# A two-layer hybrid attention trunk on one core: five changes of order and hand-over between engines

## The chip, the core and the metric

The kernel runs on one core of one Trainium2 chip. The core has a matrix engine (TensorE, PE in the profile, with its weight loads as PEld), a vector engine (VectorE, DVE), a scalar engine (ScalarE, ACT), a general engine (GpSimd, POOL) and a queue engine (SyncE, SP) that issues most of the DMA transfers. The engines run side by side and wait for each other by semaphores. The metric is the device time of one execution in microseconds (us).

## The reference, cut to what matters

Everything is float32. The sequence has 1,024 tokens, the model is 1,024 wide, and there are two layers with weights of their own.

```python
for i in range(2):                                   # DEPTH
    hn = rmsnorm(h, attn_norm[i])
    qkv = hn @ w_qkv[i]                              # 1024 x 2304
    # group A: 8 query heads, 2 key heads of 64; own chunk of 64 and the one before;
    # QK-norm, rotary on a quarter of the head, and a learned sink in the softmax
    ya = softmax(concat([scores_a, sink]))[..., :-1] @ v_a
    # group B: 8 heads of 64; own chunk and 8 before; QK-norm and a learned relative bias
    yb = softmax(scores_b + bias) @ v_b
    h = h + concat([ya, yb]) @ w_o[i]                # 1024 x 1024
    h = h + conv_gated_mlp(rmsnorm(h, ffn_norm[i]))  # up 1024 x 5632, conv of 3, silu gate, down 2816 x 1024
    gate = sigmoid(rmsnorm(h, ple_norm[i]) @ w_ple_gate[i])
    h = h + (p[i] @ w_ple_proj[i]) * gate
```

## The kernel before

A Fori loop over the two layers (L) stands on every engine, and the order of the work on each engine is written out by hand. Engines hand over by counting semaphores; a few waits name a later count than they need, by a constant at the top (C_GATE, C_HEADS and others are added to a semaphore once at the start, so that waits of the first layer have the same form). The 1,024 tokens are 8 tiles of 128 (TT), and the 1,024 columns are 8 blocks of 128 (KT). Each float32 product is three matmuls: the operands are split into a high part, which ACT writes (functions with "high"), and a low part, which DVE or POOL writes (functions with "low"), and high x high, high x low and low x high are summed in PSUM.

A layer has these stages, with their place in the first layer of the profiled span; the second layer runs about 1,293 us later.

1. Transposes of h (7 to 24 us). `transpose_x` transposes 8 x 8 tiles by matmuls with `ident` (L2001). Banks of PSUM hold four blocks; for block k at 4 or above PE waits until DVE's `x_low` (L1504) has emptied the bank of block k - 4. ACT's `x_high` (L1003) comes ahead of it. When the source is h, tiles 0 to 5 go first for blocks 0 to 3, each as soon as it is loaded; in the second layer all of them wait for the gate's last additions (L1985) of the layer before, by `s_gate_added`.
2. qkv projection (24 to 225 us), in 6 chunks of 384 columns (L2025 to L2027).
3. Attention B (225 to 355 us): 8 heads x 8 items. An item is a tile of queries of one head. Per item PE makes scores (L2134), DVE adds the bias and keeps the negated maximum (`add_bias`, L1593), ACT takes the exponential (L1098), PE transposes the probabilities (L2164), DVE or ACT copies them (L1614, L1118) and PE multiplies by v (L2183). `fill_high` and `fill_low` (L1572) make a head's q and k operands, four fills for a head of B.
4. Attention A (355 to 425 us), the same with 8 heads x 8 items. The softmax's sink: DVE adds `sink_g` and `neg_max` (L1678), ACT takes the exponential of the sum in place, and DVE's `finish` adds it to the denominator (L1628), takes the reciprocal (L1631) and scales the head's output into `qkv` (L1634).
5. Output projection (425 to 515 us): `transpose_x` of the heads' outputs once all 16 heads are done (`s_head_done`), then the products with w_o, whose rows SP loads in eight pieces (`load_o`) of 256 rows.
6. Up projection with conv and gate (515 to 965 us): products over units (L2335 to L2338); ACT and DVE put the products' results together (`c11`, `c12`, `c22`, the copy at L1395).
7. Down projection (965 to 1190 us): 42 batches of up to 24 matmuls (L2359 to L2361), whose operands `ad` and `bd` come from ACT's `ad_high`, `bd_high` (L1327, L1340) and DVE's `ad_low`, `bd_low` (L1893, L1898).
8. Gate (1190 to 1302 us): ACT's sigmoid (L1443), and DVE's product and sum into h (L1981, L1985), 16 of each, the last for tile 7.

ACT functions live in tables: `table(f)` (L973) makes a small activation that brings in the table. Here the Sqrt table comes in at the start of each layer, ahead of `x_high`.

## Time and profile before

| | |
|---|---|
| median of 3 runs (lowest, highest) | 2606.36 us (2606.30, 2608.78) |
| the profiled execution: time, span | 2602.32 us, 2600.4 us |
| PE busy, share of the span | 2551.1 us, 98% |
| PEld, DVE | 2195.6 us (84%), 1382.0 us (53%) |
| ACT, POOL | 1300.4 us (50%), 1015.2 us (39%) |
| mean granted clock of TensorE | 0.998 |
| chain that ended last | PE 93%, DVE 3%, issue 2%, ACT 1%, POOL 1% |

The span runs from the first to the last instruction of the profiled execution; its time is 1.9 us longer, and it was a little faster than the median of the three runs. Busy times are sums over all instructions of an engine, so the engine with the largest share is not at work only where that pays; the rows further down show single places.

### The profile page before, as it was taken

The numbers are of one execution on the slowest core, as the hardware profiler recorded it, in microseconds if no ns is written. First come the engines' busy times: TensorE is split into PE (matmuls) and PEld (weight loads), VectorE is DVE, ScalarE is ACT, GpSimd is POOL, SyncE is SP. The second block draws the span as 40 slices with busy tenths as digits, with TensorE's granted clock in tenths as the row PEclk, the third lists the DMA queues.
The fourth block names the chain that finished last, engine by engine and source line by source line (L and its number), as shares of the span: only waits on it lengthen the run. The fifth ranks groups of instructions, "written<-read, shape, count | busy, mean of one in ns | idle before, by whom it ended". The sixth has DMA issues, their size and how long they took to land.

```text
span 2600.4 us, 41681 instructions
## 1 busy us (share of the span) xinstructions
PE 2551.1 (98%) x13328; PEld 2195.6 (84%) x13328; DVE 1382.0 (53%) x2057; ACT 1300.4 (50%) x2156; POOL 1015.2 (39%) x749
## 2 busy tenths in 40 slices
PE   8999999999999999999999999999999999999999
PEld 8999988777888878887899999887778888788877
DVE  3114675176556567872331156742766566777732
ACT  4335775275555553333343367742755555533342
POOL 3454221238787750001124442201388787400011
PEclk9999999999999999999999999999999999999999
DMA  4111000223233248431111110003233333473312
GB/s 159 43 48 42 27 2 18 89 66 119 79 112 114 77 156 293 130 105 41 37 43 43 49 35 27 2 18 104 66 105 93 104 105 103 164 277 120 98 49 81
DMA packets 179768, 223.84 MB, mean 86 GB/s; under 512 B 7952, under 2 KB 110736, under 8 KB 179632
## 3 DMA queue, kind: packets, MB, share of 16 engines
q1 hardware_dynamic: 179040, 219.66, 26.4%
q0 software_dynamic: 592, 2.46, 0.3%
q8 instruction: 74, 1.21, 0.2%
q14 instruction: 62, 0.51, 0.1%
HBM read 169.08 MB, written 55.36 MB: 86 GB/s over the span
## 4 chain that ended last, share of the span: by engine, by line
PE 93%; DVE 3%; issue 2%; ACT 1%; POOL 1%; DMA 0%; DVEq 0%; ACTq 0%; SPq 0%; POOLq 0%
PE ps L2025 10%; PE ps L2027 10%; PE ps L2026 10%; PE ps L2335 10%; PE ps L2338 10%; PE ps L2337 10%; PE ps L2359 6%; PE ps L2361 5%; PE ps L2360 5%; PE ps L2183 5%; PE ps L2134 3%; PE ps L2164 3%; PE ps L2109 2%; PE ps L2001 1%; DMA h<-in_x 0%
## 5 line engine op out<-in xcount | busy, mean ns | idle before, releaser
L807 POOL TENSOR_TENSOR w_hl<-w_raw,w_hl 128x1024 fp32r<-128x1024 f32 x84 | 201.4, 2398 | 1039.4 <-ACT w_hl L981 1039.4
L2025 PE MATMUL ps<-w_hl,xT 128*128 128x384 f32 (+1 forms) x1280 | 461.2, 360 | 0.3
L2027 PE MATMUL ps<-w_hl,xT 128*128 128x384 f32 (+1 forms) x1280 | 460.0, 359 | 0.0
L2026 PE MATMUL ps<-w_hl,xT 128*128 128x384 f32 (+1 forms) x1280 | 460.0, 359 | 0.0
L981 ACT ACTIVATE w_hl<-w_raw 128x1024 fp32r<-128x1024 f32 x84 | 89.0, 1059 | 460.8 <-PE ps L2027 436.2
L2025 PEld LDWEIGHTS ps<-w_hl,xT 128*128 128x128 f32 x1280 | 240.2, 188 | 24.7 <-DVE xT L1504 1.5
L2027 PEld LDWEIGHTS ps<-w_hl,xT 128*128 128x128 f32 x1280 | 240.2, 188 | 23.5
L2026 PEld LDWEIGHTS ps<-w_hl,xT 128*128 128x128 f32 x1280 | 240.2, 188 | 23.3
L1836 DVE SCALAR_TENSOR_TENSOR ps<-c_up,ccols,ps 128x1023 f32<-128x1023 f32 x84 | 107.8, 1283 | 151.8 <-ACT ps L1292 151.8
L1521 DVE TENSOR_REDUCE q_sum<-sq 128x384 f32 x80 | 44.2, 553 | 271.4 <-ACT sq L1038 271.4
L1098 ACT ACTIVATE probs<-scores,neg_max 128x192 f32<-128x192 f32 (+5 forms) x256 | 144.3, 565 | 39.9 <-DVE neg_max L1593 39.3
L2359 PE MATMUL ps<-bd_two,ad 128*128 128x512 f32 x392 | 155.2, 396 | 2.8 <-DVE bd_two L1898 2.8
L1815 DVE TENSOR_TENSOR c_up<-ps,kept 128x512 f32<-128x512 f32 x126 | 86.6, 688 | 130.7 <-DMA v_rows<-hc_g 70.3
L2361 PE MATMUL ps<-bd_two,ad 128*128 128x512 f32 x392 | 154.9, 395 | 0.0
L2360 PE MATMUL ps<-bd_two,ad 128*128 128x512 f32 x392 | 154.8, 395 | 0.0
L2134 PE MATMUL ps<-ks,qs 128*128 128x192 f32 (+4 forms) x640 | 134.3, 324 | 3.1 <-DVE neg_max L1593 3.1
L1327 ACT ACTIVATE ad<-ad_raw 128x1024 fp32r<-128x1024 f32 x84 | 82.8, 986 | 105.4 <-DMA ad_raw<-v_rows 102.9
L2335 PE MATMUL ps<-x_four,ring_three 128*128 128x512 f32 x336 | 131.6, 392 | 3.4 <-POOL ring_three L919 3.4
L2335 PE MATMUL ps<-x_four,ring_four 128*128 128x512 f32 x336 | 133.2, 397 | 1.6 <-ACT kept L1251 1.5
L2338 PE MATMUL ps<-x_four,ring_four 128*128 128x512 f32 x336 | 133.0, 396 | 0.0
L2337 PE MATMUL ps<-x_four,ring_four 128*128 128x512 f32 x336 | 132.8, 395 | 0.0
L919 POOL TENSOR_TENSOR ring_four<-t_sum,ring_four 128x512 fp32r<-128x512 f32 x82 | 115.6, 1409 | 43.3 <-ACT ring_four L1178 42.1
(270 smaller groups left out, 6272.9 us busy)
## 6 DMA issues: line engine op xcount, KB each, us to landing
ad_raw<-v_rows SPq DMA_DIRECT2D x70, 512.0 KB, 3.7
raw_a<-in_w_up SPq DMA_DIRECT2D x44, 512.0 KB, 4.9
raw_g<-in_w_up SPq DMA_DIRECT2D x44, 512.0 KB, 5.2
v_rows<-c_up SPq DMA_DIRECT2D x22, 1024.0 KB, 4.4
w_raw<-in_w_qkv SPq DMA_DIRECT2D x48, 384.0 KB, 3.2
wd_main<-in_w_down SPq DMA_DIRECT2D x30, 512.0 KB, 7.8
v_rows<-hc_g SPq DMA_DIRECT2D x22, 512.0 KB, 5.0
w_raw<-in_w_o SPq DMA_DIRECT2D x16, 512.0 KB, 3.3
```

The source lines that it names most:

```text
L807: nc.gpsimd.tensor_tensor(w_hl[:, slot % 2, 1, :], w_raw[:, slot % 2, :], w_hl[:, slot % 2, 0, :].bitcast(F), ALU.subtract) \
L1098: nc.scalar.activation(buffer(probs, kind, n)[:, c0:c0 + keys], buffer(scores, kind, n)[:, c0:c0 + keys], ACT.Exp, bias=neg_max[:, hp, t:t ...
L2025: nc.tensor.matmul(dst, lhs[:, k, 0, cols], wh, start=first, stop=False)
L2026: nc.tensor.matmul(dst, lhs[:, k, 0, cols], wl, start=False, stop=False)
L2027: return nc.tensor.matmul(dst, lhs[:, k, 1, cols], wh, start=False, stop=last)
L2134: done = nc.tensor.matmul(score_bank(kind, n)[:, c:c + w], qs[:, hd % 2, t * P:(t + 1) * P], ks[:, kv(kind, hd), part, k0 + c:k0 + c + w], ...
L2335: nc.tensor.matmul(dst, wh, xs[:, 0, k], stop=False, skip_group_check=True, start=k == 0 and (q in (1, 2, 5) or (v, q) == (UNITS - 1, 4)))
L2337: nc.tensor.matmul(dst, wh, xs[:, 1, k], start=False, stop=False, skip_group_check=True)
L2338: mm = nc.tensor.matmul(dst, wl, xs[:, 0, k], start=False, stop=k == 3, skip_group_check=True)
L2359: nc.tensor.matmul(d_bank(n, t), xh[:, e, cols], wh[:, e], start=k == 0 and e == 0, stop=False)
L2360: nc.tensor.matmul(d_bank(n, t), xh[:, e, cols], wl[:, e], start=False, stop=False)
L2361: mm = nc.tensor.matmul(d_bank(n, t), xl[:, e, cols], wh[:, e], start=False, stop=k == STEPS_OF - 1)
```

## The change

It makes five edits.

- **Down's first batch.** ACT and DVE make `ad` and `bd` of batch 0 ahead of the last copy (L1395) and the last `c22` of the up projection, where they came behind them.
- **The first bias of attention.** At the start of B, DVE adds the bias of item 0 ahead of the fourth fill. At the start of A, it makes the two fills of the next head behind the biases of items 4 and 5, where they stood ahead.
- **Sink by ACT alone.** DVE's sum (L1678) goes; ACT's exponential reads `neg_max` and takes `sink_g` as its bias.
- **B rows first at the output projection.** Transposes and w_o's rows come in the order B, A. PE waits for B's heads before block 0 and for all heads only before block 3.
- **Layer boundary and table.** The Sqrt table comes in before the loop and at the end of each layer. PE starts a layer's transposes when 14 of the 16 gate additions are in, and waits for all before block 3; the early tiles take blocks 0 to 2, where they took 0 to 3.

```diff
-        C_LOW, C_USED, C_SUMS, C_HEADS, C_GATE = 2, 2, 2, 2, 2
+        C_LOW, C_USED, C_SUMS, C_HEADS, C_GATE = 2, 2, 2, 2, 4
@@ SP
                     sp.wait_ge(s_w_low_ready, L * SLOTS + i * c + (slot + 1))
+                    if O0 <= slot < P0:
+                        settled(sp)
                     sp.dma_start(dst, src).then_inc(raw_loaded[slot % 2], 16)
...
                 def load_o(j):
+                    first = 256 * ((j + 2) % 4)
@@ ACT
             act.wait_ge(s_first_loaded, 32)
+            table(ACT.Sqrt)
             with act.Fori(0, DEPTH) as L:
...
-                table(ACT.Sqrt)
                 x_high(0, 0, {1: 0, 5: 1})
...
                         if kind == "A" and t == TT - 2:
 
-                            act.wait_ge(s_den_part, L * A_HEADS + (hd + 1))
-                            nc.scalar.activation(sink_e[:, hd % 2, :], sink_e[:, hd % 2, :], ACT.Exp) \
-                                .then_inc(s_sink_exp, 1)
+                            act.wait_ge(s_scores_biased, item(hd * TT + TT - 1))
+                            nc.scalar.activation(sink_e[:, hd % 2, :], neg_max[:, hd % 2, :], ACT.Exp,
+                                                 bias=sink_g[:, hd:hd + 1], scale=1.0).then_inc(s_sink_exp, 1)
...
                 keep_s2(0, 0, last)
+                ad_high(0)
+                bd_high(0)
                 act.wait_ge(s_u_done, L * PRODUCTS + product_number(last, 7))
                 act.wait_ge(s_combined, L * COMBINED + combined_number(last, "C11"))
                 nc.scalar.activation(c_up[1][:, 0, HALF:], bank_of(last, 7), ACT.Copy).then_inc(s_kept, 1)
-                for b in range(2):
-                    ad_high(b)
-                    bd_high(b)
+                ad_high(1)
+                bd_high(1)
...
                     if n == 0:
                         high(P0 + 6)
+                table(ACT.Sqrt)
@@ DVE
                     if first and kind == "B":
-                        for f in range(len(fills(kind, 0))):
+                        for f in range(3):
                             fill_low(0, f, True)
-                        for n in range(lead_s):
+                        add_bias(0)
+                        fill_low(0, 3, True)
+                        for n in range(1, lead_s):
                             add_bias(n)
                     if first:
                         for n in range(lead_t):
                             copy_p(n)
-                        if kind == "A":
-                            for f in range(2):
-                                fill_low(1, f)
...
                             for m in within(n + lead_s):
                                 add_bias(m)
+                            if n == 0:
+                                for f in range(2):
+                                    fill_low(1, f)
...
-                        if kind == "A" and t == 4:
-
-                            dve.wait_ge(s_scores_biased, item(hd * TT + TT - 1))
-                            nc.vector.tensor_scalar(sink_e[:, hd % 2, :], neg_max[:, hd % 2, :], sink_g[:, hd:hd + 1],
-                                                    None, ALU.add).then_inc(s_den_part, 1)
...
                 c12(0, 0, last)
+                dve.wait_ge(s_combined, L * COMBINED + combined_number(last, "C12"))
+                ad_low(0)
+                bd_low(0)
                 dve.wait_ge(s_kept, L * COPIES + copy_number(last, "own"))
                 c22(0, 0, last)
-                dve.wait_ge(s_combined, L * COMBINED + combined_number(last, "C12"))
                 for b in range(BATCHES):
-                    ad_low(b)
-                    bd_low(b)
+                    if b:
+                        ad_low(b)
+                        bd_low(b)
@@ PE, transpose_x and its calls
                         ready(t)
-                        for k in range(4):
+                        for k in range(3):
                             one(t, k)
...
-                        for t in range(early if k < 4 else 0, TT):
+                        for t in range(early if k < 3 else 0, TT):
...
-                pe.wait_ge(s_gate_added, L * 2 * TT + C_GATE)
-                transpose_x(0, lambda t, k: h[:, t, k * P:(k + 1) * P],
+                def every_tile(k):
+                    if k == 3:
+                        pe.wait_ge(s_gate_added, L * 2 * TT + C_GATE)
+
+                pe.wait_ge(s_gate_added, L * 2 * TT + (C_GATE - 2))
+                transpose_x(0, lambda t, k: h[:, t, k * P:(k + 1) * P], every_tile,
...
-                pe.wait_ge(s_head_done, L * 16 + 16 + C_HEADS)
-                transpose_x(KT, lambda t, k: qkv[:, t, (k * P if k < 4 else B_Q + (k - 4) * P):
-                                                 (k * P if k < 4 else B_Q + (k - 4) * P) + P])
+                def every_head(k):
+                    if k == 3:
+                        pe.wait_ge(s_head_done, L * 16 + 16 + C_HEADS)
+
+                pe.wait_ge(s_head_done, L * 16 + B_HEADS + C_HEADS)
+                transpose_x(KT, lambda t, k: qkv[:, t, (B_Q + k * P if k < 4 else (k - 4) * P):
+                                                 (B_Q + k * P if k < 4 else (k - 4) * P) + P], every_head)
```

The program's listing shows each engine's instructions in their order; ISA and REGISTER_ALU rows belong to waits and counters. First DVE where attention B begins, before the change (L1572 is a fill, L1593 the bias of an item, whose keys are 128 for item 0 and 256 for item 1):

```order
L1572 SCALAR_TENSOR_TENSOR qs<-ps,qk_cols,qs 64x512
L1564 REGISTER_ALU
L1572 SCALAR_TENSOR_TENSOR ks<-ps,qk_cols,ks 128x512
L1572 SCALAR_TENSOR_TENSOR qs<-ps,qk_cols,qs 64x512
L1583 ISA
L1586 REGISTER_ALU
L1593 ISA scores,neg_max<-ps,bias 128x128
L1593 ISA neg_max 128x1
L1586 REGISTER_ALU
L1593 ISA scores,neg_max<-ps,bias 128x256
```

And with the change (L1576 and L1597 are the same lines there):

```order
L1576 SCALAR_TENSOR_TENSOR qs<-ps,qk_cols,qs 64x512
L1568 REGISTER_ALU
L1576 SCALAR_TENSOR_TENSOR ks<-ps,qk_cols,ks 128x512
L1587 ISA
L1590 REGISTER_ALU
L1597 ISA scores,neg_max<-ps,bias 128x128
L1597 ISA neg_max 128x1
L1576 SCALAR_TENSOR_TENSOR qs<-ps,qk_cols,qs 64x512
L1590 REGISTER_ALU
L1597 ISA scores,neg_max<-ps,bias 128x256
```

The bias of item 0 now stands ahead of the last fill; that of item 1 stands where it stood.

ACT between the up and the down projection, before (c_up is written by the copy of the last product, `ad` and `bd_two` are batch 0's operands, then `ad` and `bd_one` batch 1's):

```order
L1395 ACTIVATE c_up<-ps 128x512
L1326 REGISTER_ALU
L1327 ACTIVATE ad<-ad_raw 128x1024
L1333 ISA
L1337 REGISTER_ALU
L1340 ACTIVATE bd_two<-wd_main 128x1024
L1326 ISA
L1327 ACTIVATE ad<-ad_raw 128x1024
L1340 ACTIVATE bd_one<-wd_main 128x1024
```

With the change:

```order
L1329 ACTIVATE ad<-ad_raw 128x1024
L1335 ISA
L1339 REGISTER_ALU
L1342 ACTIVATE bd_two<-wd_main 128x1024
L1397 REGISTER_ALU
L1398 REGISTER_ALU
L1399 ACTIVATE c_up<-ps 128x512
L1328 ISA
L1329 ACTIVATE ad<-ad_raw 128x1024
L1342 ACTIVATE bd_one<-wd_main 128x1024
```

Batch 0's two activations have moved ahead of the copy and its waits.

PE at the start of a layer, before (32 transposes follow one wait; after them, 8 by 8, come those that wait for DVE's `x_low`):

```order
L1995 ISA
L2001 MATMUL ps<-ident,h 128x128 x32
L2014 ISA
L2001 MATMUL ps<-ident,h 128x128 x8
L2014 REGISTER_ALU
L2001 MATMUL ps<-ident,h 128x128 x8
```

With the change:

```order
L1999 ISA
L2005 MATMUL ps<-ident,h 128x128 x24
L2057 REGISTER_ALU
L2005 MATMUL ps<-ident,h 128x128 x8
L2018 ISA
L2005 MATMUL ps<-ident,h 128x128 x8
L2018 REGISTER_ALU
L2005 MATMUL ps<-ident,h 128x128 x8
```

A second wait (L2057, for all 16 additions) now stands behind 24 transposes, and the 8 of block 3 follow it.

## Rows read from the trace of the kernel before

**Rows 1.** PE's waits over the whole span: us in total, times, longest us

```profile
PE ps L2164 <- ACT probs L1098: 6.0, 7, 1.1
...
PE ps L2359 <- DVE bd_two L1898: 2.8, 2, 1.4
PE ps L2001 <- DVE qkv L1634: 2.6, 2, 1.3
```

**Rows 2.** Timeline of ACT, DVE and PE between up and down projection: start, duration, idle before

```profile
962.55 0.60 ACT L1395 ACTIVATE c_up<-ps 128x512 f32<-128x512 f32 x1 [4.95 <-PE ps L2338]
...
963.36 0.69 DVE L1815 TENSOR_TENSOR c_up<-ps,kept 128x512 f32<-128x512 f32 x1 [2.91 <-ACT c_up L1395]
...
965.27 1.22 DVE L1898 TENSOR_TENSOR bd_two<-wd_main,bd_two 128x1024 fp32r<-128x1024 f32 x1
...
966.63 0.47 PE L2359 MATMUL ps<-bd_two,ad 128*128 128x512 f32 x1 [1.40 <-DVE bd_two L1898]
```

**Rows 3.** DMA issues between 952 and 954.8: KB each, us to landing

```profile
ad_raw<-v_rows SPq DMA_DIRECT2D x1, 512.0 KB, 6.5
...
wd_main<-in_w_down SPq DMA_DIRECT2D x1, 512.0 KB, 6.2
```

**Rows 4.** Timeline of DVE and PE at the start of attention B

```profile
226.62 0.76 DVE L1572 SCALAR_TENSOR_TENSOR qs<-ps,qk_cols,qs 64x512 fp32r<-64x512 f32 x1 [0.73 <-ACT qs L1051]
...
227.77 0.62 PE L2134 MATMUL ps<-ks,qs 128*128 128x384 f32 x2 [1.53 <-DVE neg_max L1593]
...
229.06 0.44 PE L2164 MATMUL ps<-ident,probs 128*128 128x128 f32 x2
```

**Rows 5.** Timeline of DVE and PE at the start of attention A

```profile
356.87 1.43 DVE L1572 SCALAR_TENSOR_TENSOR qs<-ps,qk_cols,qs 64x512 fp32r<-64x512 f32 x2
358.32 0.42 DVE L1593 CUSTOM_DVE_ANT_0 scores<-ps,mask_a,neg_sink 128x192 f32<-128x192 f32 x1
...
359.38 0.88 PE L2164 MATMUL ps<-ident,probs 128*128 128x128 f32 x4 [1.14 <-ACT probs L1098]
```

**Rows 6.** The sink's sum by its line (ns min/median/max), and POOL's timeline at the first long one

```profile
L1678 DVE TENSOR_SCALAR sink_e<-neg_max,sink_g x16: 220/230/1950, 363.8 to 1715.8; 128x8 f32<-128x8 f32 x16
...
363.78 1.91 POOL L815 TENSOR_TENSOR q_nat<-qkv,q_rstd 128x1024 f32<-128x1024 f32 x1 [4.00 <-PE ps L2109]
```

**Rows 7.** Timeline of PE where three heads of attention A begin their products with v

```profile
386.32 0.88 PE L2183 MATMUL ps<-qkv,probsT 128*128 128x64 f32 x6 [0.33 <-DVE probsT L1614]
...
395.93 0.88 PE L2183 MATMUL ps<-qkv,probsT 128*128 128x64 f32 x6 [0.34 <-DVE probsT L1614]
...
404.19 0.88 PE L2183 MATMUL ps<-qkv,probsT 128*128 128x64 f32 x6 [0.34 <-DVE probsT L1614]
```

**Rows 8.** Stretches of A: length, busy PE, PEld, DVE, ACT, POOL, PE clock, DMA

```profile
1653.60:1657.10 3.50, 3.50 (x20) 3.50 (x19) 1.20 (x6) 1.01 (x2) 0.00 (x0) 0.51 0.00 0
...
359.38:368.03 8.65, 7.27 (x60) 6.40 (x60) 6.65 (x18) 5.40 (x19) 2.31 (x2) 1.00 0.00 1
1652.30:1661.21 8.91, 8.58 (x59) 7.96 (x60) 4.93 (x18) 5.42 (x19) 2.31 (x2) 0.81 0.00 1
```

**Rows 9.** Timeline of DVE and PE at the boundary of the layers

```profile
1300.57 0.69 DVE L1985 TENSOR_TENSOR h<-gate_s,h 128x512 f32<-128x512 f32 x1
...
1310.32 2.48 DVE L1504 SCALAR_TENSOR_TENSOR xT<-ps,ncols,xT 128x1024 fp32r<-128x1024 f32 x2 [6.19 <-ACT xT L1003]
...
1304.19 5.38 PE L2001 MATMUL ps<-ident,h 128*128 128x128 f32 x32 [2.31 <-DVE h L1985]
...
1316.97 0.44 PE L2025 MATMUL ps<-w_hl,xT 128*128 128x384 f32 x1
```

**Rows 10.** The loop's jump: ACT's timeline behind it; branches (ns min/median/max, first and last start)

```profile
1304.66 1.28 ACT L973 ACT_TABLE_LOAD   x1 [1.98 <-issue]
...
L976 ACTq COMPARE_BRANCH  x2: 40/42/45, 1302.1 to 2595.2; - x2
...
L1464 DVEq FUSED_REGOPS  x2: 63/65/67, 3.8 to 1306.6; - x2
```

More of the change, by code:

```diff
@@ L547, in trunk @@
         s_sinks_set = sem("sinks_set")
-        s_den_part = sem("den_part")
         s_sink_exp = sem("sink_exp")
@@ L642, in load_o @@
                 def load_o(j):
+                    first = 256 * ((j + 2) % 4)
                     load(O0 + j, 0, 0, rows2(O0 + j, HALF),
-                         tiled(w_o[ds(L, 1), 256 * (j % 4):256 * (j % 4) + 256, j // 4 * HALF:(j // 4 + 1) * HALF]))
+                         tiled(w_o[ds(L, 1), first:first + 256, j // 4 * HALF:(j // 4 + 1) * HALF]))
                 load_o(0)
```

## The prediction

> **What bounds the kernel now.** The first view read is the page's head: PE is busy 98% of the span and holds 93% of the chain that ended last. An edit therefore pays only where PE is idle or runs at its lower clock. The second is PE's waits by cause: single waits of 1.1 to 1.4 us [rows 1] and one of 2.3 between the layers [rows 9], most of them once a layer, where PE waits on another engine's order of work. The third is the timeline of the waiting engines ahead of each such wait: which instruction released PE, and what stood ahead of it. The fourth is the table of stretches, for the granted clock. The sum is made against the profiled execution (2602.32 us, span 2600.4) and then taken off the median, 2606.36 us, which is 4.0 us longer.
>
> **1. Down's first batch.** PE's first down matmul comes 1.40 us late, released by DVE's `bd_two` at 965.27 + 1.22 = 966.49 [rows 2]. That chain begins with ACT's copy at 962.55, a copy that waits 4.95 us for PE; DVE too sits idle for 2.91 us before 963.36. So both engines have free time before PE ends its last product at about 965.2 (966.63 less 1.40). The only question is whether the operands are there. Batch 0's `ad_raw` is issued after 952 and lands 6.5 us later; its weights are issued before 954.8 and land 6.2 us later, before 961 [rows 3]. With ACT's two activations (about 1 us each; the order listing puts them ahead of the copy) and DVE's two at 1.22, both parts are done by about 964.1 even if DVE starts only at 961.7. The wait goes: 1.40 in each layer, 2.8 together, as PE's waits give it for two times [rows 1]. Next late is batch 1, which DVE now makes behind `c22`, as before; a batch of 24 matmuls of 0.47 us that overlap by about half (an estimate) lasts over 5 us, so batch 1's operands, which DVE begins right behind `c22`, have some slack. **2.8 us.**
>
> **2. First bias of B.** PE waits 1.53 us at 227.77 for the bias of item 0, which stands on DVE behind a fill of 0.76 that itself came 0.73 late behind ACT [rows 4]. The order listing shows that bias moved ahead of the fill, but the bias of item 1 not. So the bias of item 0 comes 1.3 to 1.5 earlier, the upper bound. But PE's transposes of item 1 at 229.06 hang on the bias of item 1, behind the fill as before, which only saves the bias ahead of it (0.2 to 0.3), and on ACT, which then has item 0 out of its way. I take 0.5 (between 0.3 and 1.5, near the lower end, as one item alone cannot keep PE busy). **1.0 us** for two layers.
>
> **3. First bias of A.** Two fills of 1.43 us in all stand at 356.87 ahead of the bias at 358.32, and PE waits 1.14 us at 359.38 [rows 5]. With the fills behind, the bias begins at 356.87; ACT is then busy with a copy until about 357.75, so its exponential and PE's transposes come 1.05 earlier (bounds 0.6 and 1.14). The fills belong to the next head, so their new place costs nothing while that head is several us away. **2.1 us** for two layers.
>
> **4. The sink's sum.** It is 16 instructions of a median of 0.23 us on DVE, with a longest of 1.95 [rows 6]. Three are long, and the first stands right beside POOL's 1.91 us at 363.78 [rows 6]. The 13 short ones lie in idle time of DVE and cost PE nothing. A long one shows in PE's pace: the head starts at 386.32, 395.93 and 404.19 are 9.61 and 8.26 us apart [rows 7]; the first interval holds a long sum, the second none, so one costs 1.35 (lower bound 1.0, PE's idle time there by itself). What replaces it on ACT is nothing: the exponential was there before, with one wait fewer ahead of it. **4.05 us** for three.
>
> The Trainium skill (SBUF — State Buffer, SBUF: two separate sides) says that DVE and GpSimd share a pair of ports which one of them holds for a whole instruction while the other blocks. The trace agrees (1.95 against 0.23), and by that rule a sum that is gone can't collide, but another DVE instruction may meet POOL's in its place; that is rival 2.
>
> **5. The clock in layer 1's A.** TensorE's granted clock stands at its lower level (0.51, that is 1.2 GHz) from 1653.60 to 1657.10 [rows 8], right after PE's idle 1.1 us at the start of A. The same work takes 8.91 us there, and 8.65 in layer 0, where it holds one long sum [rows 8]: 8.65 − 1.35 = 7.30, so the fall costs 1.6. In layer 0 the same idle time brought no fall, so it is a matter of chance; with the idle time gone I take it as gone. **1.6 us** (bounds 0 and 1.6).
>
> **6. B rows first at the output projection.** PE waits 1.3 us, twice, for the last head's scaled output [rows 1]. B's heads are long done, so blocks 0 to 2 (24 transposes, about 2.7 us) need no wait, and only block 3 does, by then met. ACT's and DVE's copies of the transposed blocks begin as much earlier; ACT's table and DVE's last scaling are done by then. w_o's pieces change only their rows; the first two are loaded during B. SP's added instruction is one of tens of ns per load. **2.6 us.**
>
> **7. Layer boundary.** Here everything between PE's last gate matmul and its first qkv matmul at 1316.97 is a chain. Before: DVE's last addition, PE's transposes at 1304.19 after 2.31 us of waiting, DVE's first `x_low` at 1310.32, first product 6.65 after that [rows 9]. PE would now start after the addition for tile 5 (1300.57 + 0.69 = 1301.26) and its own last matmul, which ends at 1304.19 − 2.31 = 1301.88: 2.3 earlier. `x_high` needs its bank, and `x_low` needs DVE. ACT compares for its jump at 1302.1 and does its first instruction behind it, the table load of 1.28 us, at 1304.66; DVE is back in the loop only at 1306.6 [rows 10]. Neither DVE's jump nor its start moves. The table load now stands ahead of ACT's jump, from about 1302.7; the likelier case is that the jump's 2.5 us run beside it, since compare and fetch are the sequencer's work. So ACT's `x_high` can be done before 1306, and DVE's first `x_low` comes at about 1306.8 instead of 1310.3. From there on the chain has five `x_low` of 1.24 (2.48 for two [rows 9]), so the first product comes at about 1313.1: **3.9 us**, once. The lower value: if ACT's jump begins only when the table is in, at about 1304.0, its 2.5 us end near 1306.4, `x_high` and with it `x_low` come some 1.2 later, and 2.7 us are won.
>
> The Trainium skill (Runtime: NRT & Kernel Launch, Instruction fetch mechanics) states that a taken branch out of the window of fetched pages forces a transfer of the target page before execution goes on. The trace agrees: 2.5 us from compare to the next instruction on ACT. By that rule a table load ahead of the jump could not be hidden by it, and the sum would be 1.2 us smaller.
>
> The first layer's start has nothing to win, since x comes by DMA there; the table load before the loop lies beside that load, and the one at the end of the last layer beside the last stores.
>
> **Sum.** 2.8 + 1.0 + 2.1 + 4.05 + 1.6 + 2.6 + 3.9 = 18.05 us, so 2602.32 falls to about 2584.3 and the median, 2606.36, to 2588.3. That is 0.7%; 0.2% (5.2 us) is about what a measurement of this kernel can tell from no change.
>
> **The rivals.** *Forecast, all of it about as summed:* a gain of 15 to 20.5 us, 2586 to 2591.5. Its bounds are items 2, 3 and 7 at their lower values together (−0.4, −0.9, −1.2) and item 2 at its upper one (+2). Chance 0.58.
>
> *Rival 1: the boundary gives its gain back.* PE has a new gap there: it ends 32 transposes before DVE is back, so it is idle for some 2 us, and at the same kind of place the clock stood at its lower level for 3.5 us at a price of 1.6 [rows 8]. With the late jump (−1.2) and one such fall in the first products (−1.6 more): 18.05 − 2.8 = 15.2, some 2591. For it: the boundary has three engines' jumps in it. Against it: the chain there is bound by DVE and not by PE's clock until the first product. Chance 0.19.
>
> *Rival 2: the collisions move, and the fall stays.* POOL's instruction now meets another of DVE's small ones (reciprocal or sum of the denominator). Then the 4.05 and the 1.6 stay lost: 12.4 us, 2594. For it: POOL's work is placed by the same events as before, a few tenths of a us from DVE's. Against it: none of those was long in the 16 heads before, only the sink's sum. Chance 0.13.
>
> *Rival 3: waits replaced by waits.* Each wait removed uncovers one behind it, on DMA, say w_o's rows or `ad`'s second batch. If only the sink's part stays, the gain is 4 us, 2602, within 0.2%. Against it: the copies behind each wait have slack in the timeline. Chance 0.07.
>
> *Rival 4, the other side: the clock.* In A, PE has gaps (7.27 us busy of 8.65 [rows 8]). If the new spacing of its work let the clock fall to its lower level in A again and again, each fall of 3.5 us costs 1.6. Slower by over 0.2% needs 18.05 + 5.2 = 23.3 us, or 15 such falls in 16 heads; at 8 falls the gain would be 5 us and lost in the noise. One fall is in the trace, and the change makes the gaps fewer. Chance 0.03, slower and a little below that together.
>
> **How the numbers follow.** The likeliest case gives 2588.3. The range goes from 2584 (item 2 at its upper value, and 2 us for sizes of mine that are short) to 2596, which takes in rivals 1 and 2; what is left out above is rivals 3 and 4 at 0.10. Faster by over 0.2% (below 2601.1) are the forecast, rivals 1 and 2 and a little of 3: 0.91. Within 0.2%: the rest of 3 and the small side of 4, 0.07. Slower: 0.02.
>
> **What the profile after would show.** Item 1: no wait of PE on `bd_two`. Items 2 and 3: the wait on `neg_max` at 227.8 shorter, but a short one on item 1's exponential left; the 1.14 at the start of A gone or under 0.2. Item 4: no DVE instruction of 1.9 us in A, head intervals all 8.3. Item 5: clock 1.00 through layer 1's A. Item 6: the transposes from `qkv` follow the last product with v at once. Item 7: from the end of PE's last gate matmul to the first qkv matmul 11.2 us in place of 15.1 (1301.88 to 1316.97), and DVE, not ACT, ahead of `x_low`. Wrong would make it: long instructions of DVE under other names, w_o's load late at the output projection, or the lower clock in more than one stretch of A.

## The result and the profile after

The median of four executions is 2583.39 us (2583.16 to 2583.57), beside 2607.24 us for the kernel before (2606.30 to 2608.78): a measured ratio of 0.9899, interval [0.9881, 0.9917] (the two medians by themselves give 0.9909, inside it). The forecast was 2588.3 with a range of 2584 to 2596, so the time fell 0.6 us below the range. The profiled execution went from 2602.32 to 2583.39 us, 18.93 less, where 18.05 had been summed. Taken off 2606.36, even 18.93 gives 2587.4, inside the range. The step that failed is therefore not in the sum but behind it: the median moved by 23.0 from the 2606.36 that the prediction started from, and by 23.9 from 2607.24. Some of this was luck: run again, the changed kernel has a median of 2587.1, inside the range and 1.2 below the forecast (see the experiments).

PE's waits over the whole span of the changed kernel (us in total, times, longest us; its line numbers are 4 to 12 higher). The waits on `bd_two`, on `qkv` and on h's last addition are gone, and those on ACT's exponential fell from 6.0 to 0.6 [rows 1]:

```profile
PE ps L2191 <- DVE probsT L1618: 3.3, 10, 0.3
...
PE ps L2142 <- DVE neg_max L1597: 1.5, 4, 0.5
...
PE ps L2172 <- ACT probs L1100: 0.6, 2, 0.3
```

Timeline of PE at the start of B, the start of A, in A, at the output projection, and at down's first batch (start, duration, idle before and its releaser):

```profile
228.49 0.44 PE L2172 MATMUL ps<-ident,probs 128*128 128x128 f32 x2
...
357.64 0.88 PE L2172 MATMUL ps<-ident,probs 128*128 128x128 f32 x4
...
383.22 0.88 PE L2191 MATMUL ps<-qkv,probsT 128*128 128x64 f32 x6 [0.33 <-DVE probsT L1618]
...
391.49 0.88 PE L2191 MATMUL ps<-qkv,probsT 128*128 128x64 f32 x6 [0.34 <-DVE probsT L1618]
...
420.59 1.15 PE L2005 MATMUL ps<-ident,qkv 128*128 128x128 f32 x9
...
959.25 0.39 PE L2371 MATMUL ps<-bd_two,ad 128*128 128x512 f32 x1
```

Read against [rows 2, 4, 5, 7], the same rows stood at 229.06, 359.38, 386.32, 395.93 and 966.63. The lead is 0.57 us behind the first bias of B (0.19 of it from the program's start), 1.74 behind the first bias of A, 3.10 and 4.44 each time that a long sum is gone, and 7.38 behind the output projection and down together. The transposes at 420.59 follow the last product with v without a gap.

Timeline of ACT and DVE at down's first batch. The last operand of batch 0 is ready at 957.39 (956.17 + 1.22), ahead of PE's start at 959.25, and ACT's copy comes behind ACT's part of it:

```profile
955.07 1.07 ACT L1342 ACTIVATE bd_two<-wd_main 128x1024 fp32r<-128x1024 f32 x1 [0.80 <-DMA wd_main<-in_w_down]
...
956.73 0.60 ACT L1399 ACTIVATE c_up<-ps 128x512 f32<-128x512 f32 x1 [0.59 <-PE ps L2350]
...
956.17 1.22 DVE L1899 TENSOR_TENSOR bd_two<-wd_main,bd_two 128x1024 fp32r<-128x1024 f32 x1 [0.17 <-ACT bd_two L1342]
```

Timeline at the boundary of the layers, and the rows of ACT's and DVE's jump (ns min/median/max, first and last start):

```profile
1294.28 3.66 PE L2005 MATMUL ps<-ident,h 128*128 128x128 f32 x32
...
1300.69 5.23 PE L2005 MATMUL ps<-ident,h 128*128 128x128 f32 x32 [2.76 <-DVE xT L1508]
1305.68 0.42 PE L2029 MATMUL ps<-w_hl,xT 128*128 128x384 f32 x1
...
1295.18 1.28 ACT L975 ACT_TABLE_LOAD   x1
...
L979 ACTq FUSED_REGOPS  x2: 50/53/56, 3.0 to 1297.2; - x2
...
L979 ACTq COMPARE_BRANCH  x2: 40/42/45, 1294.5 to 2576.4; - x2
...
1299.35 6.05 DVE L1508 SCALAR_TENSOR_TENSOR xT<-ps,ncols,xT 128x1024 fp32r<-128x1024 f32 x5 [2.74 <-ACT xT L1006]
...
L1468 DVEq FUSED_REGOPS  x2: 63/65/67, 3.0 to 1299.1; - x2
```

PE starts its transposes with no wait at all. ACT's jump runs from 1294.5 to 1297.2, and the table load lies inside it: ACT's sequencer and its table load ran side by side, so the prediction's likelier case held, and its rule that a table load ahead of the jump could not be hidden by it did not. DVE is back at 1299.1 and starts `x_low` 0.25 us later, in one run of five. From the end of PE's last gate matmul (1294.44) to the first qkv product it is 11.2 us, as forecast; it was 15.1. Not all of that is the edit's: 1.6 us of it was a fall of the clock in the execution before, as shown further down.

One collision in each layer did move, as rival 2 had it, to the sum of the denominator (L1632, at 392.07 and 1673.87; L1628 before, whose longest was 0.17). It takes 0.78 us, and behind it the lead shrinks by 0.15 and 0.18 us:

```profile
L1632 DVE TENSOR_TENSOR den<-den,sink_e x16: 154/164/779, 365.5 to 1702.7; 128x8 f32<-128x8 f32 x16
```

### The profile page after: what moved, and what is told of

Its sections match the earlier page's. It is cut to its first block, busy times and chain, and to the rows that moved or that the text cites. A ratio compares the mean times of both kernels' runs of the same rounds, so it can differ in the third digit from the quotient of the medians.

```text
span 2581.5 us, 41681 instructions
## 1 busy us (share of the span) xinstructions
PE 2546.2 (99%) x13328; PEld 2191.5 (85%) x13328; DVE 1375.0 (53%) x2041; ACT 1303.0 (50%) x2158; POOL 1015.4 (39%) x749
## 4 chain that ended last, share of the span: by engine, by line
PE 93%; DVE 2%; issue 2%; ACT 1%; POOL 1%; DMA 0%; ACTq 0%; DVEq 0%; SPq 0%; POOLq 0%
PE ps L2029 10%; PE ps L2031 10%; PE ps L2030 10%; PE ps L2347 10%; PE ps L2350 10%; PE ps L2349 10%; PE ps L2371 6%; PE ps L2373 6%; PE ps L2191 6%; PE ps L2372 6%; PE ps L2142 3%; PE ps L2172 3%; PE ps L2117 2%; PE ps L2005 1%; DMA h<-in_x 0%
```

## The experiments

Eighteen runs were made, two of them of the unchanged kernels, most with 6 or 12 executions each. They ran in five groups, each on a chip of its own, and the kernel before ran beside each group (its median went from 2606.0 to 2613.2 us between them), so a kernel is best compared with the one before of its own group, as the ratio does. In the table, the clock is the mean over executions of the mean granted clock. Over all groups the kernel before has 122 executions: 2602.0 to 2626.0, median 2609.8, clock 0.9954.

| kernel | n | lowest, median, highest us | clock | ratio to before, interval |
|---|---|---|---|---|
| before, again | 12 | 2602.4, 2608.9, 2618.8 | 0.9959 | 0.9995 [0.9972, 1.0018] |
| changed, again | 6 | 2583.5, 2587.1, 2587.4 | 0.9993 | 0.9903 [0.9882, 0.9924] |
| sink alone | 12 | 2596.7, 2600.5, 2606.9 | 0.9978 | 0.9972 [0.9953, 0.9991] |
| bias of A alone | 12 | 2603.8, 2612.1, 2617.5 | 0.9950 | 1.0002 [0.9982, 1.0023] |
| boundary alone | 12 | 2598.6, 2603.5, 2614.5 | 0.9963 | 0.9982 [0.9961, 1.0003] |
| B's rows alone | 12 | 2600.3, 2607.5, 2617.5 | 0.9953 | 0.9988 [0.9970, 1.0006] |
| down alone | 12 | 2601.3, 2612.0, 2621.5 | 0.9934 | 0.9995 [0.9975, 1.0016] |
| sink and bias of A | 7 | 2595.1, 2597.4, 2602.0 | 0.9971 | 0.9935 [0.9912, 0.9958] |
| changed, sink's sum on DVE | 12 | 2590.7, 2596.5, 2607.5 | 0.9964 | 0.9950 [0.9933, 0.9967] |
| changed, old boundary | 6 | 2586.0, 2591.1, 2594.6 | 0.9987 | 0.9925 [0.9903, 0.9946] |
| changed, old bias of A | 6 | 2585.3, 2589.5, 2591.1 | 0.9992 | 0.9901 [0.9874, 0.9927] |
| changed, old rows | 6 | 2586.7, 2590.0, 2595.1 | 0.9995 | 0.9914 [0.9894, 0.9934] |
| changed, old bias of B | 6 | 2583.9, 2586.9, 2590.0 | 0.9988 | 0.9904 [0.9885, 0.9923] |
| changed, old down | 6 | 2590.0, 2590.7, 2594.2 | 0.9992 | 0.9918 [0.9900, 0.9937] |
| changed, DVE stalls | 12 | 2606.8, 2610.7, 2617.4 | 0.9933 | 0.9989 [0.9968, 1.0009] |
| changed, ACT stalls of 0.8 | 6 | 2587.3, 2591.0, 2595.0 | 0.9995 | 0.9918 [0.9898, 0.9938] |
| changed, ACT stalls of 1.2 | 6 | 2588.1, 2592.6, 2598.0 | 0.9985 | 0.9934 [0.9916, 0.9952] |
| changed, ACT stalls of 3.1 | 12 | 2612.2, 2614.7, 2618.6 | 0.9919 | 1.0017 [1.0004, 1.0030] |

### Spread: the kernel before and the changed one, again

No edit.

> The kernel before, unchanged, as a measure of how its executions spread. Theory C (clock): the timed executions lie above the profiled one of 2602.3 because they hold one to three more stretches at the lower TensorE clock (each 1.6 to 1.7 us), which follow PE's waits; expected: times from 2601 to 2609 in steps of about 1.7, and a lower mean clock (0.996 to 0.997) where the time is longer. Theory E (execution): the offset has nothing to do with the clock; expected: times near 2606 to 2608 at the same clock of 0.998 as the profiled one.

> The changed kernel, unchanged, for its spread. Theory P (phase): the qkv projection of a layer runs at one of two paces, 0.1733 or 0.1766 us from matmul to matmul, 3.8 us apart per layer, drawn anew in each execution, and the clock's falls come on top; the change doesn't touch the draw, and the first result (2583.2 to 2583.6) was the lucky end: expected 2583 to 2600, median 2587 to 2589, as far above the profiled execution as before. Theory R (removed): the change takes away what starts the slow pace and most falls; expected 2583 to 2586 in nearly all executions, median 2583.5, while the kernel before spreads from 2602 to 2620 on the same chip.

Measured: over all groups the kernel before spreads over 24 us, with a mean clock from 0.989 to 0.999 and longer times at a lower clock. So theory E, that the times differ at the same clock, is refuted; theory C, that the longer times come with a lower clock, holds, but its range, 2601 to 2609, is too short. The profiled execution here has four falls ahead of the end. Three of its stretches (length, busy PE, PEld, DVE, ACT, POOL, PE clock, DMA share, GB/s) are just behind waits of PE: the start of A, in A, and the output projection:

```profile
361.30:364.70 3.40, 3.40 (x19) 3.40 (x17) 1.49 (x6) 1.64 (x5) 0.00 (x0) 0.50 0.00 0
1689.10:1692.50 3.40, 3.40 (x19) 3.38 (x18) 1.62 (x6) 1.08 (x5) 0.00 (x0) 0.51 0.40 149
1719.80:1723.20 3.40, 3.40 (x17) 3.40 (x18) 0.34 (x1) 1.02 (x1) 0.00 (x0) 0.50 0.00 0
```

The changed kernel has a second thing that varies and is not the clock. Its profiled execution, 2587.36 us, has not one fall before its end, and is 3.97 us longer than the first one. Nearly all of the two layers' qkv projections, the same 1,151 matmuls, shows why:

```profile
24.13:223.24 199.11, 199.11 (x1151) 199.07 (x1152) 39.38 (x71) 77.89 (x125) 88.56 (x89) 1.00 0.20 56
1305.84:1508.75 202.91, 202.91 (x1152) 202.87 (x1153) 39.38 (x71) 78.40 (x126) 88.72 (x89) 1.00 0.18 50
```

Both at full clock and fully busy, but 3.80 us apart. Per matmul that is 0.1730 us in one and 0.1763 in the other. Of the 40 layers in the 20 profiled executions of this study, 11 ran at the slow pace, in the first layer or in the second, in kernels of both kinds.

So each theory was half right. The pace is drawn in the changed kernel too (theory P, 2583.5 or 2587.3), and the clock's falls are nearly gone from it (theory R). The six times fit it: two at 2583.5 and 2584.4, four at 2587.0 to 2587.4, as with no slow layer and with one. All of the first four executions, at 2583.2 to 2583.6, were of the first kind, and that was luck.

### Single parts on the kernel before

The sink alone, the bias of A alone, the boundary with the table alone, B's rows alone, and down alone. Each is the hunks of the change that belong to it; the core of each:

```diff
# sink
+                            nc.scalar.activation(sink_e[:, hd % 2, :], neg_max[:, hd % 2, :], ACT.Exp,
+                                                 bias=sink_g[:, hd:hd + 1], scale=1.0).then_inc(s_sink_exp, 1)
# bias of A
+                            if n == 0:
+                                for f in range(2):
+                                    fill_low(1, f)
# boundary and table
+                pe.wait_ge(s_gate_added, L * 2 * TT + (C_GATE - 2))
# B's rows
+                pe.wait_ge(s_head_done, L * 16 + B_HEADS + C_HEADS)
# down
+                ad_high(0)
+                bd_high(0)
```

> Only the sink's sum is left to ACT. By the profiled sum: 4.05 us less, 2603 beside a median of 2607. Theory C adds what falls of the clock follow the collisions of DVE with POOL: 1.6 to 3.3 us more if they cause some, none if they don't. Rival (collisions move to another small DVE instruction): 0 us, and a DVE instruction of 1.9 us under another name in A.

> Only the two fills at the start of A move behind the biases. By the profiled sum: 2.1 us less (1.05 in each layer) and 1.6 more for the clock's fall behind the wait in layer 1. Theory C: the fall at the start of A comes in many executions of the kernel before, up to one in each layer, so 3.7 to 5.4 us less in the median. Theory E: 2.1 us less.

> Only the layer boundary: 14 of 16 additions waited for, blocks 0 to 2 early, table load ahead of the jump. By the sum: 3.9 us less. If one of the two stretches of lower clock at the boundary also goes, its price lies in transposes that wait for DVE anyway, so still about 3.9. If ACT's jump begins only behind the table load: 2.7.

> The kernel before with only B's rows first at the output projection and w_o in that order. By the sum 2.6 us less than before (profile: PE's wait of 1.3 on the last head's output gone, twice). Rival: w_o's rows or the last copies late, with a wait at the first product of w_o; 0 to 1 us less. The clock fell at this place in other executions, so 1.6 more may go in each layer.

> The kernel before with only down's first batch made ahead. By the profile 2.8 us less (PE's wait of 1.40 gone in both layers). No fall of the clock was seen at this place, so the mean clock stays at that of the kernel before, 0.9957, and the best executions come to 2599. Rival (the wait moves to batch 1): 0 to 1 us less.

Measured: the profile shows each removed wait gone, but against a spread of 24 us only the sink alone is told from no change in the times: its median lies 5.6 below, where 4.05 was expected (the interval allows both), and its clock rises from 0.9957 to 0.9978. The other lowest times are 0.8 to 3.5 us below before's 2602.1, except the bias of A alone, whose lowest is 2603.8. Its profiled execution (2613.23) shows why it can't be read in the times: seven falls and one layer at the slow pace. Theory C is refuted where it gave the falls to the wait at the start of A alone; there are as many without it.

### Two parts together

The sink and the bias of A (the two diffs above).

> The kernel before with two parts, the sink's sum on ACT and the biases of A first, which leaves no wait of PE over 0.4 us inside attention A. By the profile 4.05 + 2.1 = 6.2 us less than before's executions with the same clock. Theory W (the clock falls where PE has waits of a us and more in attention): hardly a fall left in A, mean clock 0.998 to 0.999, median 2594 to 2597. Rival (each part acts by itself, and bias_a alone took no fall away): clock as with the sink alone, 0.9978, median 2598.

Measured: the lowest is 2595.1, as summed (6.2 below 2602.1 is 2595.9), and the clock, 0.9971, not above the sink's alone. That is the rival's outcome; theory W had 0.998 to 0.999. The four falls of its profiled execution are at 19.8, 422.5, 1518.2 and 1712.8 us, none inside A, but three of them where waits are left: the start of B, and the end of A in both layers.

### Single parts taken out of the changed kernel

```diff
# changed kernel with the sink's sum on DVE again
+                            nc.vector.tensor_scalar(sink_e[:, hd % 2, :], neg_max[:, hd % 2, :], sink_g[:, hd:hd + 1],
+                                                    None, ALU.add).then_inc(s_den_part, 1)
# with the old boundary
-                pe.wait_ge(s_gate_added, L * 2 * TT + (C_GATE - 2))
+                pe.wait_ge(s_gate_added, L * 2 * TT + C_GATE)
# with the old bias of A: fill_low(1, f) ahead of the loop again
# with the old rows
+                pe.wait_ge(s_head_done, L * 16 + 16 + C_HEADS)
# with the old bias of B: four fills, then the biases
# with the old down: ad_high(0), bd_high(0), ad_low(0), bd_low(0) behind the copy and c22
```

> The changed kernel with the sink's sum back on DVE. By the profile 4.05 us more than the changed kernel (2587.5 in the best executions), if the sum still meets POOL's instruction three times; the number of long sums may change as the other parts shift it: 1.35 for each. If collisions bring falls of the clock (theory R), the spread grows to that of the kernel before; by theory P it doesn't change.

> The changed kernel with the layer boundary and the table load as before. By the profile 3.7 us more (2587.1 in the best executions). Theory R, if the boundary's wait of 2.3 us and its clock fall start the slow pace in layer 2: executions at 2591 appear, 3.8 above. Theory P: as many slow executions as the changed kernel has.

> The changed kernel with the two fills again ahead of the first biases of A: PE waits 1.14 us at the start of A, 2.1 us more in the two layers (2585.5 in the best executions). Theory W: one wait in each layer brings up to one fall of 1.6 us behind it, so times up to 2589, and 3.8 more where the slow pace is drawn. Rival: a single wait brings no fall, clock 0.999 to 1.0.

> The changed kernel with A's and B's rows in the old order at the output projection: PE waits 1.3 us there again, 2.6 in all by the profile. Falls were seen just behind this wait (422 to 425, 1713 to 1720 us). Theory W: mean clock 0.998 to 0.999, 1.6 more in some executions; rival: clock as the changed kernel, 0.9993.

> The changed kernel with the old order at the start of B: PE waits 1.53 us there again, but by the trace only 0.9 us come back for both layers (0.37 and 0.51). Falls were seen behind this place (228.6, 1518 to 1531 us). Theory W: up to 1.6 more in some executions, so this edit is worth more in the median than its 0.9; rival: clock as the changed kernel.

> The changed kernel with down's first batch in the old order: PE waits 1.40 us again, 2.8 to 3.3 us more in all. No fall was ever seen at this place, so both theories expect the changed kernel's clock, and 2586.5 or, with the slow pace in one layer, 2590.3. If falls appear here, the place doesn't matter, only the wait.

Measured: taking out the sink's part is the only one that brings the spread back, 17 us of it, and the clock down to 0.9964. In its profile the long sums are four, not three: which heads meet POOL shifts with the rest. Its lowest, 2590.7, is 7.2 above the changed kernel's, where 4.05 was expected: four sums are 5.4, and one fall of 1.6 would make up the rest. Four of the five others cost in their lowest time about what was summed (over 2583.5: 1.8 bias of A, 3.2 rows, 0.4 bias of B, and with 2.5 a little less at the boundary), and the clock falls little or not at all: 0.9987, 0.9992, 0.9995, 0.9988, 0.9992. In these kernels a single wait of 1.1 to 1.3 us at the start of A or at the output projection brought hardly a fall. For the boundary and the bias of B, with six executions each, 0.0005 of clock is too little to say; but the profile of the old bias of B has one fall, and it stands right behind the wait that was put back in the first layer:

```profile
228.14 0.62 PE L2140 MATMUL ps<-ks,qs 128*128 128x384 f32 x2 [1.53 <-DVE neg_max L1597]
...
230.00:233.40 3.40, 3.40 (x18) 3.20 (x16) 2.14 (x5) 2.65 (x7) 3.40 (x4) 0.50 0.00 0
```

The length of a wait doesn't decide alone. The wait of 1.31 us at the output projection has a fall beside it in both layers of the profiles of the sink alone and of the two parts, and in none of the profile of the old rows. The wait of 1.40 us at down's first batch stands 16 times in the eight profiles that have it, and no fall is behind any of them. What else decides was not tested.

The boundary cost 2.5 us in the lowest time where 3.7 was expected; the reason is in the section on the prediction. All six of old down lie at 2590.0 or above, which fits 2.8 to 3.3 us of wait plus one slow layer; the profiled one is such a case, for the others it is argued. The highest would be those with both layers slow.

### Stalls by DVE, and by ACT

The question left is what brings the falls: PE's waits, or the meeting of DVE with POOL. Four waits were put into the changed kernel, in heads 0 and 3 of A of both layers. First by DVE:

```diff
+                        if kind == "A" and t == 4 and hd in (0, 3):
+                            nc.vector.tensor_tensor(junk[:, 1, :], h[:, 0, :], h[:, 0, :], ALU.mult)
+                            nc.vector.tensor_tensor(junk[:, 0, 0:HALF], h[:, 1, 0:HALF], h[:, 1, 0:HALF], ALU.mult)
```

> The changed kernel, and in heads 0 and 3 of attention A DVE makes two products of 1.9 us together that nobody reads, where the sum stood that met POOL. The work of the output isn't touched. By the profile each stall holds PE up by about 1.35 us: 4 x 1.35 = 5.4 more, 2589 in the best executions. Theory W: PE's waits themselves bring the falls: clock 0.996 to 0.998 and a spread of 2589 to 2605, as with the sink's sum on DVE. Rival (the falls hang on the sink's sum or its meeting with POOL): clock stays at 0.999 to 1.0 and the times at 2589 to 2593.

Measured: 23 us lost for four stalls in the lowest time and 24 in the median, against the changed kernel run again. The clock, 0.9933, lies below the range of both theories. The stalls were larger than meant, since the second product itself met POOL (2.40 us; an operation of that size takes 0.7), so this kernel doesn't separate the two. PE's row behind the first stall, DVE's second product, and the stretch behind:

```profile
366.69 1.13 PE L2175 MATMUL ps<-ident,probs 128*128 128x128 f32 x4 [2.62 <-ACT probs L1100]
...
363.21 2.40 DVE L1683 TENSOR_TENSOR junk<-h 128x512 f32<-128x512 f32 x1
...
366.20:376.50 10.30, 9.73 (x46) 9.18 (x47) 6.07 (x21) 5.36 (x19) 0.00 (x0) 0.51 0.01 2
```

Then by ACT, ahead of the exponentials, in three sizes (the first two differ in the copies; the third makes two of the second's, one behind the other):

```diff
+                        if kind == "A" and t == 4 and hd in (0, 3):
# 0.8 us
+                            nc.scalar.activation(junk[:, 0, :], h[:, 0, :], ACT.Copy)
+                            nc.scalar.activation(junk[:, 1, 0:HALF], h[:, 1, 0:HALF], ACT.Copy)
# 1.2 us
+                            nc.scalar.activation(junk[:, :, :], h[:, 0:2, :], ACT.Copy)
```

> The changed kernel, and in heads 0 and 3 of attention A ACT makes two copies (about 1.7 us together) that nobody reads, ahead of the exponentials; the output's work is untouched. DVE and POOL have nothing added. Each stall should hold PE up by 1 to 1.5 us, four times: 4 to 6 us by itself. Theory W (PE's waits bring the falls, whoever makes PE wait): mean clock 0.995 to 0.998 and 1.6 us more for each fall, 2590 to 2600. Rival (it is DVE's meeting with POOL that brings them): clock 0.999 to 1.0, 2588 to 2593 with the pace's 3.8 in it.

> As after_with_act_stalls, with one copy of 2,048 columns on ACT (about 1.9 us) in heads 0 and 3: PE should wait 1.0 to 1.1 us there, as it does after the sink's long sum, without DVE or POOL. Without falls the times are 2583.5 plus 4 x 1.35 = 2589, and 3.8 more for each layer with the slow pace. Theory W: clock 0.996 to 0.998, 2591 to 2602. Rival (the meeting of DVE and POOL): clock 0.9995, 2589, 2593 or 2597.

> The same with two such copies one behind the other (about 3.8 us): PE should wait 2.6 to 3 us there, as with the stalls of DVE that brought ten falls. Without falls 2583.5 plus 4 x 3.2 = 2596.5 (plus the pace). Theory W: about two to three falls behind each stall, clock 0.993 to 0.995, 2606 to 2615. Rival: clock 0.9995, 2596 to 2604.

Measured: the waits of PE were 0.82, 1.16 and 3.10 us, four of each, with nothing added to DVE or POOL. At 0.82, shorter than meant, no fall: the clock is 0.9995, as the rival had it, and the six times stand at 2587.3 to 2587.6, 2590.8 to 2591.2 and 2594.9 to 2595.0, which fit zero, one and two layers at the slow pace, 3.8 apart. At 1.16 the clock is 0.9985, between the two theories' values, with one execution at 0.996; the profiled one has a stretch at the lower clock as long as two falls, behind its fourth stall. At 3.10 it is 0.9919, a little below theory W's range: four stretches in the profiled execution, as long as ten falls together, one at each stall, two of them beginning while PE still waits. PE's rows of the last two, with one stretch behind a stall of each:

```profile
363.67 0.88 PE L2174 MATMUL ps<-ident,probs 128*128 128x128 f32 x3 [1.16 <-ACT probs L1100]
...
1677.60:1684.40 6.80, 6.80 (x36) 6.80 (x34) 3.69 (x14) 2.76 (x12) 1.01 (x1) 0.50 0.25 80
```

```profile
365.51 1.13 PE L2177 MATMUL ps<-ident,probs 128*128 128x128 f32 x3 [3.10 <-ACT probs L1101]
...
364.70:374.90 10.20, 9.39 (x44) 9.13 (x45) 4.42 (x14) 5.29 (x20) 0.00 (x0) 0.50 0.01 2
398.80:409.00 10.20, 9.80 (x47) 9.55 (x47) 4.42 (x14) 4.87 (x19) 1.17 (x1) 0.50 0.17 53
```

With 3.1 us by ACT the falls come as with 2.6 us by DVE. So long waits of PE in attention A bring them, whoever makes PE wait; the meeting of DVE with POOL is not needed. That waits are all there is to the sink's sum is not shown: its four waits in the profile are 1.04 us each, and its clock is 0.9964, where four waits of 1.16 by ACT leave 0.9985. Whether its place in the head, some 2 us later, or its meeting with POOL adds to it was not separated. Behind the wait the clock can stay down for 6.8 or 10.2 us, although PE is busy in nearly all of that time.

## Why the prediction was right, and where it failed

The steps, each measured as the growth of the changed kernel's lead at the same matmul in the two profiled executions:

| term | forecast us | measured us |
|---|---|---|
| down's first batch, 2 layers | 2.8 | 3.3 (1.63, 1.64) |
| first bias of B, 2 layers | 1.0 | 0.7 (0.38, 0.36) |
| first bias of A, 2 layers | 2.1 | 2.3 (1.17, 1.17) |
| three collisions | 4.05 | 4.05 (1.35, 1.34, 1.35) |
| the fall in layer 2's A | 1.6 | 1.6 |
| B's rows first, 2 layers | 2.6 | 2.7 (1.37, 1.34, less the moved collisions) |
| layer boundary | 3.9 | 3.9, of which 1.6 a fall |
| sum | 18.05 | 18.6, with 0.2 at the program's start and 0.1 at its end to 18.9 |

Every step came within half a us of its number, and all but the last were right in mechanism too. Down gave 0.24 more per layer than its wait of 1.40; why is not shown.

**Step 7, the boundary, hit its number by luck.** The prediction put the whole way from DVE's first `x_low` at 1310.32 to 1306.8 down to the new order. But the profiled execution of before has a fall of the clock in PE's first 32 transposes, which take 5.38 us [rows 9]:

```profile
1305.50:1308.80 3.30, 3.30 (x17) 3.30 (x16) 0.00 (x0) 0.64 (x2) 0.00 (x0) 0.50 0.01 2
```

The same kernel again, without a fall there (its last gate matmul ends at 1302.31):

```profile
1304.62 3.71 PE L2001 MATMUL ps<-ident,h 128*128 128x128 f32 x32 [2.31 <-DVE h L1985]
...
1309.20 2.48 DVE L1504 SCALAR_TENSOR_TENSOR xT<-ps,ncols,xT 128x1024 fp32r<-128x1024 f32 x2 [4.63 <-ACT xT L1003]
...
1315.85 0.45 PE L2025 MATMUL ps<-w_hl,xT 128*128 128x384 f32 x1
```

From the last gate matmul to the first qkv product that is 13.5 us in place of 15.1. With the old order the eight profiles have 13.5 five times, without a fall in these transposes, and 15.1 to 15.2 three times, with one. With the new order the twelve have 10.9 to 11.7. So the new order by itself is worth about 2.3 us, and 1.6 of the 3.9 is a second fall of the profiled execution, which the prediction didn't see. As these falls begin in or just behind PE's wait of 2.31 us, and none of the twelve has one in its first 32 transposes, the edit may take them away too; at three in eight that would be 0.6 more on average (an estimate). The changed kernel with the old boundary says the same: 2.5 in its lowest time. That such a fall would cost nothing, since the transposes wait for DVE anyway, was expected of the boundary alone. It holds for the later transposes (from DVE's first `x_low` to the first product it is 6.65 us in both, with a fall at 1312.3 in one and none in the other), not for the first 32.

**The step that failed** is the one that carried the sum to the result: the sum was made against the profiled execution "and then taken off the median, 2606.36 us, which is 4.0 us longer". That took the 4.0 as a constant that both kernels have. It isn't one. The profiled execution of before was near the lower end of its executions: 2602.3, where 122 of them have a median of 2609.8. What lies above is falls of the clock, about 1.6 us each where PE is the engine that is waited for, and the slow pace, 3.8 us a layer. The mean clock of before, 0.9954, is 0.0046 x 2600 = 12 us of full clock that are missing, some seven falls at 1.7 (half of 3.4) each; its profiled execution (0.998) had four. The changed kernel's two had two and one. In each case one of them is at the very end, as in all profiles. By their times, the changed kernel's first four executions had no slow layer, so all of them lay at the foot. In the six repeated ones four had one, and their median, 2587.1, is within the range: the gap to the forecast is in part the missing falls, which the change took away, and in part the draw of the pace.

**Step 5** saw a fall behind a wait, and had the wrong scale. It called the fall "a matter of chance" and priced the one in the trace, 1.6 us; in the mean over executions there are some six more than in the changed kernel. **Step 4** named only the 1.35 us of each collision. The runs show that the sink's part carries most of the falls too: 0.9957 to 0.9978 when it is put in alone, 0.9993 to 0.9964 when it is taken out. In the profiled pair that is hidden; the medians move by 5.6 us when it is put in alone, and by 9.4 when it is taken out. **Rival 4** looked at the very mechanism, but only with its sign turned: it asked whether the change would bring more falls, not how many of them the kernel before had.

Of the other rivals, rival 1's late jump did not come about (the table load lay inside ACT's jump), and the new idle time of PE at the boundary, 2.76 us, did carry one fall, at 1300.4, but in front of transposes that wait for DVE anyway:

```profile
1300.40:1303.80 3.40, 3.11 (x15) 3.11 (x16) 3.40 (x4) 3.06 (x4) 2.37 (x1) 0.51 0.00 0
```

An execution without it is no shorter (2587.36 less the slow pace's 3.80 is 2583.56). Rival 2 came true in one place in each layer and cost 0.15 and 0.18 us. Rival 3 did not happen: nothing stood behind the removed waits.

Which of the four first executions of before had a slow layer is not known; two at 2606.3 are 3.8 above 2602.5, which would fit one, but this is only argued. What draws the pace is open as well. It was not tried.

## What to carry to other kernels

A single profiled execution prices a removed wait of TensorE well, but it is one draw: it can lack stretches at half clock that other executions have, and it can hold one inside the very chain that is being priced, as at the boundary here. So run both kernels several times, look at the granted clock of each, look for a fall inside each chain before pricing it, and add the expected number of falls behind the waits that the change removes. And when a kernel spreads over 24 us, judge an edit of 1 to 4 us by the lead at the same instruction in two traces and by the lowest times, not by medians of a dozen.

## What the runs showed of the hardware that was not expected

- Four waits of PE of 0.8 us in attention A brought no fall of its clock, four of 1.2 us a few (mean clock 0.9985), four of 3.1 us ten (0.9919); the stretches last 3.4, 6.8 or 10.2 us at 1.2 in place of 2.4 GHz, and one of 3.4 cost 1.6 us in attention A, and as much in the first transposes at the boundary. Behind 16 waits of 1.40 us at down's first batch there was none.
- The same 1,151 matmuls of the qkv projection take 199.1 or 202.9 us in a layer, at full clock and with no wait, and which it is changes with the layer and the execution (11 layers of 40 at the slower pace).
- On ACT, the loop's jump of 2.7 us and a table load of 1.28 us ran at the same time.
